# The recurrence's state products on the full array with zero blocks, and new places for buffers in SBUF

## The chip, the cores and the metric

One core of one Trainium2 chip runs the whole program. The time is the device time in microseconds, as the median of three runs. One execution more was taken with the hardware profiler, and the rows below come from it.

## The reference

Two blocks of a language model, in float32, over 256 tokens of width 2048. What matters here is the first block's recurrence (16 heads of 64, run as 8 pairs) and the large weight matrices around it.

```python
h = rms_norm(x, g_mix); proj = h @ w_in            # first projection, 60 units of 128 columns
y_dsa = dsa_mixer(q, k, v, q_idx, k_idx, w_idx)    # attention over selected keys
# recurrence, per head, over tokens t (state is 64 x 64)
def step(state, inp):
    sa = einsum('bhvk,bhk->bhv', state, -kk_t)
    state = state * w_t + sa[..., None] * b_t + v_t[..., None] * k_t
    return state, einsum('bhvk,bhk->bhv', state, r_t)
x = x + concat([y_dsa, y_rwkv]) @ w_out
x = x + hier_moe(rms_norm(x, g_ffn), ...)          # 16 experts, 2 of a group per token
# second block: projection, gates, three mixers, three branches, MLP with 4 * 2048 hidden
```

## The kernel before, in words

**Weights.** They come in units of 128 x 2048 floats through four ring slots (and, in the experts, two more). Each unit is split in two parts of fewer bits: ScalarE rounds it to a high part (`half_high`, L653, and `split_high`, L692), VectorE subtracts for the low part, in place (`half_low`, L658, and `split_low`, L699). The features are split likewise. A product of weights and features is three matmuls: high x high, high x low, low x high, 48 for a unit of 16 k-steps. Where the weights are loaded into the array and 256 columns of features stream, this is `split_unit` (L797, L799, L800) or, in the first projection, `product` (L855, L856, L857). Where the features are loaded and 512 columns of weights stream, it is `tokens_unit` (L823 to L825) and the expert products.

**Places.** All of this lies in one piece of SBUF that is taken by order: `ring`, `HT`, `YT`, `XT`, `C`, `SQ`, `work`. High parts of weights lie in `work`, `C`, `SQ` or `YT`, low parts in their slot. Features lie in `HT`, `YT`, `XT` or `work`. `H2_HI` and `H2_LO`, the MLP's input, lie in `work`.

**The recurrence.** It is done in chunks of 64 tokens, four for each of 8 pairs of heads. `pair(p)` on TensorE first makes scores, then inverts a triangular matrix by blocks (`sq2` to `inv64`), and then walks over the chunks c: `W` (state and keys), `U` (the inverse times W), `Z` (the change of the state), and the outputs of the chunk. Each is a product per head of 64 x 64, so two per pair, on the upper and the lower half of the array. W and U are copied by ScalarE (L1651, L1653) before the next product reads them. Z is taken by VectorE (L2236, L2238). `low_rank` makes the next pair's decays and gate (L896 to L899).

**The order.** It is written out by hand: `PE_RW`, `ACT_RW` and `DVE_RW` list the steps; each engine's queue follows them, and one semaphore per engine counts them. After each step TensorE runs a share of the first projection (`fill`), so that the wait for ScalarE or VectorE is covered. The shares are in `FILL`, 2 where none is given, and a cumulative sum turns them into whole k-steps, 96 for a pair (288 matmuls). When such a fill ends a half unit, ScalarE and VectorE have to round the next one, in their queues' order (`round_ahead`, `follow`). GpSimd does nothing until the first projection's later units are taken, then rotary products and, in the second block, tables.

Of the kernel before, what the change touches and what calls it, by code (L numbers as in the profile page):

```python
# [7 lines left out]
F32R = mybir.dt.float32r  # L8
# [291 lines left out]
FILL.update({f"{s}{c}": 1 for s in "WU" for c in range(NCH)})  # L300
FILL_FIRST = {"lora": 5, "kks": 14}
# [18 lines left out]
def build(nc, A, out):  # L320
    ctx = ExitStack()
    with ctx:
# [14 lines left out]
        ONEKA = sb("ONEKA", [P, 8])  # L337

        def split_memory(kind, suffix, pieces):
# [4 lines left out]
            shapes += [(f"work{i}", [P, n]) for i, n in enumerate(pieces)]  # L344
            with ExitStack() as c:
                return [c.enter_context(nc.sbuf_tensor(n + suffix, shape, kind)) for n, shape in shapes]
# [3 lines left out]
        def split_places(kind, suffix, pieces):  # L350

            shapes = [("ring", [P, RING, UNIT]), ("HT", [P, KT, T]), ("YT", [P, KT, T]), ("XT", [P, KT, T]),
                      ("C", [P, NC]), ("SQ", [P, 4, T])]
            shapes += [(f"work{i}", [P, n]) for i, n in enumerate(pieces)]
            with ExitStack() as c:
                return [c.enter_context(nc.sbuf_tensor(n + suffix, shape, kind)) for n, shape in shapes][6:]
# [3 lines left out]
        _, XG = split_places(F32R, "_tokens", [2 * PIECE, TILES * PIECE])  # L360
        PG = ctx.enter_context(nc.psum_tensor("PG", [P, BANKS, 512], F32))
# [78 lines left out]
        pool_chain = sem("pool_chain")  # L440
        g_in, g_sq, g_sum, g_ms, g_rt, g_vn, g_t, g_tt, g_mix, g_y = (sem("gmlp_" + n) for n in (
# [23 lines left out]
        ZB = cube(area(2 * CH), 2)  # L465
        ZP, W_, U_ = (area(CH) for _ in range(3))
        Y_, YC = area(T), area(T)
        ENDS = area(NCH)
        YSQ, G_IN = KK2, DA.rearrange("p n a -> p (n a)")
# [74 lines left out]
        GT = cube(area(3 * KT * T), 3 * KT)  # L544
        W_HI2_AT = taken[0]
# [3 lines left out]
        PW = [area(S5_TILES) for _ in range(5)]  # L549
        NEGM = area(P)  # L550
# [27 lines left out]
        H2_HI, H2_LO = rounded(gates_at + 2 * KT * T, KT), rounded(gates_at + KT * T, KT)  # L578
# [193 lines left out]
        def _(pe):  # L772
# [130 lines left out]
            def pair(p):  # L903
# [68 lines left out]
                for c in range(NCH):  # L972
# [35 lines left out]
                    if c + 1 == NCH:  # L1008
                        done(mm, p, f"Z{c}")
# [2005 lines left out]
```

## Time and profile before

| | us |
|---|---|
| median of three runs (lowest to highest) | 3074.66 (3071.51 to 3075.66) |
| profiled execution, its own time | 3069.26 |
| its span, first to last instruction | 3067.5 |
| TensorE, VectorE, ScalarE, GpSimd busy | 2964.6, 1918.2, 1532.9, 161.9 |

PE is TensorE's matmuls, PEld its weight loads, which overlap them; DVE is VectorE, ACT ScalarE and POOL GpSimd. A float32 product is recorded as two matmuls. Matmul durations overlap, so the start of the next one is what shows a product's price.

### The profile page before, as it was taken

Reading aid. Unit: us, or ns where it says so; the run is one execution under the profiler, and the core shown is the slowest. Engines: PE = TensorE matmul, PEld = TensorE weight load, DVE = VectorE, ACT = ScalarE, POOL = GpSimd, SP = SyncE. Lnnn points to the kernel's source line nnn. Section 1 sums busy time; section 2 is a strip of 40 time slices with the busy share of each in tenths; the row PEclk is TensorE's granted clock in tenths of the full one; section 3 lists DMA queues with packets and bytes.
Section 4 is the critical chain, followed back from the end, with each engine's and each line's share of the span. In section 5 each row is a group of like instructions: output and inputs, shape, how many; then the busy total and the mean of one; then the engine's idle time right before and its main releaser. Section 6 shows DMA issues by size and latency. Waiting matters only on the chain.

```text
span 3067.5 us, 52890 instructions
## 1 busy us (share of the span) xinstructions
PE 2964.6 (97%) x22088; PEld 2643.6 (86%) x22088; DVE 1918.2 (63%) x2591; ACT 1532.9 (50%) x2132; POOL 161.9 (5%) x248
## 2 busy tenths in 40 slices
PE   8999999879899999999899999999999999999998
PEld 7888888767688887777899999999989989898996
DVE  6555555874777877877759954445665545555454
ACT  5445444454566666665543347654344434344443
POOL 0000000200000000000075500000000000000000
PEclk9999999989899999999999999999999999999999
DMA  6223233223688888877444444445545555555554
GB/s 235 88 107 111 98 111 111 75 107 110 234 318 315 324 319 303 325 297 266 152 165 166 152 160 171 165 174 211 192 181 201 188 187 191 188 184 191 189 183 150
DMA packets 81955, 582.46 MB, mean 190 GB/s; under 512 B 9024, under 2 KB 9280, under 8 KB 12480
## 3 DMA queue, kind: packets, MB, share of 16 engines
q1 hardware_dynamic: 79056, 566.45, 50.0%
q10 hardware_dynamic: 2672, 12.71, 1.1%
q8 instruction: 175, 2.87, 0.4%
q14 instruction: 52, 0.43, 0.1%
HBM read 574.93 MB, written 4.19 MB: 189 GB/s over the span
## 4 chain that ended last, share of the span: by engine, by line
PE 86%; DVE 9%; ACT 2%; issue 1%; DMA 0%; ACTq 0%; SPq 0%; DVEq 0%
PE PG L799 10%; PE PG L797 10%; PE PG L800 10%; PE PG L824 6%; PE PG L825 6%; PE PG L823 6%; PE PG L855 4%; PE PG L1242 4%; PE PG L1243 4%; PE PG L1244 4%; PE PG L856 3%; PE PG L857 3%; DVE ring_r L699 3%; PE PX L942 2%; PE PX L1294 1%
## 5 line engine op out<-in xcount | busy, mean ns | idle before, releaser
L699 DVE TENSOR_TENSOR ring_r<-ring,work_r 128x1024 fp32r<-128x1024 f32 x492 | 584.0, 1230 | 313.8 <-ACT work_r L692 312.6
L692 ACT ACTIVATE work_r<-ring 128x1024 fp32r<-128x1024 f32 x492 | 493.0, 1051 | 537.8 <-PE PG L800 290.6
L692 ACT ACTIVATE C_r<-ring 128x1024 fp32r<-128x1024 f32 x268 | 269.1, 1052 | 419.1 <-PE PG L800 295.5
L800 PE MATMUL PG<-YT_r,ring_r 128*128 128x256 f32 x1664 | 469.1, 282 | 0.0
L699 DVE TENSOR_TENSOR ring_r<-ring,C_r 128x1024 fp32r<-128x1024 f32 x268 | 319.6, 1234 | 214.4 <-ACT C_r L692 213.2
L800 PE MATMUL PG<-work_r,ring_r 128*128 128x256 f32 x1344 | 374.8, 279 | 0.0
L800 PEld LDWEIGHTS PG<-YT_r,ring_r 128*128 128x128 f32 x1664 | 315.7, 190 | 0.0
L857 PE MATMUL PG<-HT_r,ring_r 128*128 128x256 f32 x960 | 271.1, 282 | 0.0
L800 PEld LDWEIGHTS PG<-work_r,ring_r 128*128 128x128 f32 x1344 | 253.3, 189 | 0.0
L824 PE MATMUL PG<-ring_r,HT_r 128*128 128x512 f32 x624 | 246.9, 396 | 0.0
L797 PE MATMUL PG<-YT_r,C_r 128*128 128x256 f32 x832 | 237.6, 286 | 6.4 <-DVE ring_r L699 6.4
L797 PE MATMUL PG<-YT_r,work_r 128*128 128x256 f32 x832 | 235.7, 283 | 5.9 <-DVE ring_r L699 5.9
L799 PE MATMUL PG<-HT_r,C_r 128*128 128x256 f32 x768 | 217.2, 283 | 0.0
L799 PE MATMUL PG<-HT_r,work_r 128*128 128x256 f32 x768 | 216.1, 281 | 0.0
L797 PE MATMUL PG<-work_r 128*128 128x256 f32 x672 | 188.8, 281 | 0.0
L797 PE MATMUL PG<-work_r,C_r 128*128 128x256 f32 x672 | 187.0, 278 | 0.0
L857 PEld LDWEIGHTS PG<-HT_r,ring_r 128*128 128x128 f32 x960 | 182.6, 190 | 0.0
L799 PE MATMUL PG<-work_r 128*128 128x256 f32 x640 | 179.8, 281 | 0.0
L799 PE MATMUL PG<-work_r,C_r 128*128 128x256 f32 x640 | 178.1, 278 | 0.0
L797 PEld LDWEIGHTS PG<-YT_r,C_r 128*128 128x128 f32 x832 | 159.5, 192 | 8.1 <-issue 7.6
L797 PEld LDWEIGHTS PG<-YT_r,work_r 128*128 128x128 f32 x832 | 158.9, 191 | 7.5 <-issue 7.0
L855 PE MATMUL PG<-HT_r,YT_r 128*128 128x256 f32 x480 | 153.7, 320 | 11.7 <-DVE XT_r L2040 11.7
(649 smaller groups left out, 7138.3 us busy)
## 6 DMA issues: line engine op xcount, KB each, us to landing
ring<-weights SPq DMA_DIRECT2D x472, 1024.0 KB, 4.8
C<-weights SPq DMA_DIRECT2D x32, 1024.0 KB, 4.8
work<-weights SPq DMA_DIRECT2D x32, 1024.0 KB, 5.1
work<-xT SPq DMA_DIRECT2D x4, 512.0 KB, 7.1
XT<-x ACTq DMA_DIRECT2D x1, 2048.0 KB, 10.0
residual<-XT ACTq DMA_DIRECT2D x4, 512.0 KB, 3.0
XT<-residual ACTq DMA_DIRECT2D x1, 2048.0 KB, 11.9
result<-YT SPq DMA_DIRECT2D x8, 256.0 KB, 2.9
```

The costliest lines, as they stand in the source:

```text
L692: act.activation(w_high(u)[:, c], weights(u)[:, c], ACT.Copy).then_inc(w_hi, 1)
L699: dve.tensor_tensor(w_low(u)[:, c], weights(u)[:, c], w_high(u)[:, c].bitcast(F32), ALU.subtract).then_inc(w_lo, 1)
L797: pe.matmul(o, wh, high[:, k, :], start=(n == 0 and not (down and t_ % 2)), stop=False, skip_group_check=True)
L799: pe.matmul(o, wh, low[:, k, :], start=False, stop=False, skip_group_check=True)
L800: last = pe.matmul(o, wl, high[:, k, :], start=False, stop=(n == kts - 1), skip_group_check=True)
L823: pe.matmul(o, xh, wh, start=(first and kk == 0), stop=False, skip_group_check=True)
L824: pe.matmul(o, xh, wl, start=False, stop=False, skip_group_check=True)
L825: mm = pe.matmul(o, xl, wh, start=False, stop=(last and kk == 3), skip_group_check=True)
L855: pe.matmul(o, wh, HT_r[:, k, :], start=(k == 0), stop=False, skip_group_check=True)
L857: mm = pe.matmul(o, wl, HT_r[:, k, :], start=False, stop=(k == KT - 1), skip_group_check=True)
L1242: pe.matmul(o, xh, wh, start=(k == 0), stop=False, skip_group_check=True)
L1243: pe.matmul(o, xh, wl, start=False, stop=False, skip_group_check=True)
```

## The change

1. W, U and Z of a chunk are each one product on 128 rows for both heads. The loaded operand is 128 x 128 with the two heads' 64 x 64 blocks on the diagonal and zeros elsewhere: `ARD`, `BTOKD`, `KTOKD`, `MKD`, `QD`. GpSimd clears these once at the start and copies the blocks for each pair; `QD` is written by VectorE, in two instructions for the last step of the inverse. TensorE waits for the copies before `W0`.
2. The outputs stay on 64 x 64 parts. Those of chunks 0, 1 and 2 are made after `W3`, those of chunk 3 as the last step. States `ZB` and `U_` are kept for all chunks. `FILL["W3"]` is 0.
3. The second product of the gate (`GUP`) loads all 128 rows in place of 32; the rows added are zero.
4. Gaps between buffers, and places of its own for the MLP's input; `PW` and `NEGM` move.

```diff
+FILL["W3"] = 0
+        sb("gap", [P, 8])
+        GAPS = (208, 0, 0, 48, 0, 176)      # floats before HT, YT, XT, C, SQ, work
+        H2_REST = 208
+        _, H2_LO_, H2_HI_ = split_places(F32R, "_hidden", [4 * PIECE + H2_REST, PIECE, PIECE])
-        H2_HI, H2_LO = rounded(gates_at + 2 * KT * T, KT), rounded(gates_at + KT * T, KT)
+        H2_LO, H2_HI = (cube(a, KT) for a in (H2_LO_, H2_HI_))
...
-                done(pe.matmul(PX[:, 2, T:2 * T], GUP[0:32, 1, cols], LO[0:32, 2, :], ...), p, "lora")
+                done(pe.matmul(PX[:, 2, T:2 * T], GUP[:, 1, cols], LO[:, 2, :], ...), p, "lora")
...
                 for c in range(NCH):
                     if c == 0:
                         dve(p, "q64")
+                        pe.wait_ge(s_blocks, 3 * p + 3)
                     else:
                         dve(p, f"z{c - 1}")
-                        for hs in HEADS:
-                            pe.matmul(PX[hs, 0, 0:CH], AR[hs, tt, 0, cs], z[hs, :], start=True, stop=False)
-                    for hs in HEADS:
-                        mm = pe.matmul(PX[hs, 0, 0:CH], MKK[hs, c, 0, :], VTOK_[hs, c, :], ...)
-                    done(mm, p, f"W{c}")
+                        pe.matmul(PX[:, 0, 0:CH], ARD[:, c - 1, :], ZB[:, c - 1, :], start=True, stop=False)
+                    done(pe.matmul(PX[:, 0, 0:CH], MKD[:, c, :], VTOK_[:, c, :], ...), p, f"W{c}")
+                    if c + 1 == NCH:
+                        for before in range(c):
+                            outputs(before)
                     act(p, f"W{c}")
-                    for hs in HEADS:
-                        mm = pe.matmul(PX[hs, 1, 0:CH], Q_[hs, c, :], W_[hs, :], start=True, stop=True)
+                    done(pe.matmul(PX[:, 1, 0:CH], QD[:, c, :], W_, start=True, stop=True), p, f"U{c}")
                     act(p, f"U{c}")
                     if c + 1 < NCH:
+                        pe.matmul(PX[:, 2, 0:CH], BTOKD[:, c, :], U_[:, c, :], start=True, stop=False)
+                        done(pe.matmul(PX[:, 2, 0:CH], KTOKD[:, c, :], VTOK_[:, c, :], ...), p, f"Z{c}")
+                    else:
+                        done(outputs(c), p, f"Z{c}")
...
+                    for h, hs in enumerate(HEADS):
+                        ins = dve.tensor_tensor(QD[hs, :, h * CH:h * CH + CH], Q_[hs], bank(b)[hs], ALU.add)
+                    done(ins, p, "q64")
...
         def _(pool):
+            for n, blocks in enumerate((ARD, BTOKD, KTOKD, MKD, QD)):
+                pool.memset(blocks, 0.0).then_inc(s_empty, 1)
+            pool.wait_ge(s_empty, 5)
+            for p in range(MT):
+                pool.wait_ge(DR.sem, DR.at(p, "ar"))       # then 4 copies into ARD
+                pool.wait_ge(AR_.sem, AR_.at(p, "tok"))    # then 4 copies into BTOKD, KTOKD
+                pool.wait_ge(DR.sem, DR.at(p, "mk"))       # then 2 copies into MKD
```

## Rows read from the trace of the kernel before

**Rows 1.** The page, part 1: busy us, share of the span, instructions.

```profile
PE 2964.6 (97%) x22088; PEld 2643.6 (86%) x22088; DVE 1918.2 (63%) x2591; ACT 1532.9 (50%) x2132; POOL 161.9 (5%) x248
```

**Rows 2.** TensorE in time in the fourth pair: start us, us, line, out<-in; W0, U0, Z1.

```profile
270.88 0.33 PE L984 MATMUL PX<-work 64*64 64x64 f32 x4
271.14 0.39 PE L855 MATMUL PG<-HT_r,YT_r 128*128 128x256 f32 x1
271.36 0.28 PE L856 MATMUL PG<-XT_r,YT_r 128*128 128x256 f32 x1
...
271.84 0.28 PE L857 MATMUL PG<-HT_r,ring_r 128*128 128x256 f32 x1
272.05 0.33 PE L988 MATMUL PX<-work 64*64 64x64 f32 x4
...
273.44 0.33 PE L993 MATMUL PX<-work 64*64 64x64 f32 x4 [0.51 <-ACT work L1653]
...
273.82 0.39 PE L855 MATMUL PG<-HT_r,work_r 128*128 128x256 f32 x1
```

**Rows 3.** ScalarE in time beside it: copy of W, rounding of a half unit.

```profile
271.26 0.23 ACT L1651 ACTIVATE work<-PX 128x64 f32<-128x64 f32 x1 [2.04 <-PE PX L984]
272.22 1.06 ACT L653 ACTIVATE YT_r<-ring 128x1024 fp32r<-128x1024 f32 x1 [0.73 <-PE PG L857]
```

**Rows 4.** TensorE in time: the gate's two products, and a product alone in the fill.

```profile
276.45 0.70 PE L898 MATMUL PX<-work 128*128 128x256 f32 x2
...
277.71 0.39 PE L855 MATMUL PG<-HT_r,work_r 128*128 128x256 f32 x1
...
278.88 0.60 PE L901 MATMUL PX<-work,C 128*128 128x256 f32 x2
...
279.44 0.28 PE L856 MATMUL PG<-XT_r,SQ_r 128*128 128x256 f32 x1
```

**Rows 5.** TensorE in time, experts: float32 records on the full array with few columns.

```profile
812.51 1.50 PE L1213 MATMUL PX<-work,work_r 128*128 128x5 f32 x12
813.87 0.48 PE L1242 MATMUL PG<-HT_r,work_tokens 128*128 128x512 f32 x1
```

**Rows 6.** VectorE in time, fourth pair: step "mk", and the inverse's last sum.

```profile
249.40 0.76 DVE L2203 TENSOR_TENSOR work<-PX,C 128x256 f32<-128x256 f32 x2 [0.99 <-PE PX L924]
...
269.37 0.42 DVE L2225 TENSOR_TENSOR work<-work,PX 128x256 f32<-128x256 f32 x1 [1.46 <-PE PX L942]
```

**Rows 7.** Groups of GpSimd: count, busy us, mean ns, idle before; its copies.

```profile
L2877 POOL COPY work<-work 128x32 f32<-128x32 f32 x1 | 1.2, 1183 | 943.5 <-DVE work L2635 943.5
...
L2884 POOL COPY XT<-work 128x32 f32<-128x32 f32 x2 | 0.5, 240 | 0.1
```

**Rows 8.** TensorE in time: starts of units of 48 products, gates and MLP.

```profile
2049.73 0.28 PE L797 MATMUL PG<-YT_r,work_r 128*128 128x256 f32 x1
...
2055.38 0.28 PE L797 MATMUL PG<-YT_r,C_r 128*128 128x256 f32 x1
...
2061.14 0.28 PE L797 MATMUL PG<-YT_r,work_r 128*128 128x256 f32 x1
...
2351.15 0.28 PE L797 MATMUL PG<-work_r,C_r 128*128 128x256 f32 x1
...
2356.59 0.28 PE L797 MATMUL PG<-work_r 128*128 128x256 f32 x1
...
2362.24 0.28 PE L797 MATMUL PG<-work_r,C_r 128*128 128x256 f32 x1
...
2529.02 0.28 PE L797 MATMUL PG<-work_r,C_r 128*128 128x256 f32 x1
...
2551.64 0.28 PE L797 MATMUL PG<-work_r,C_r 128*128 128x256 f32 x1
```

**Rows 9.** TensorE in time: end of a unit whose products stream 512 columns.

```profile
2338.84 0.40 PE L825 MATMUL PG<-work_r,HT_r 128*128 128x512 f32 x1
2339.07 0.28 PE L797 MATMUL PG<-work_r,C_r 128*128 128x256 f32 x1
```

More of the change, by code:

```diff
@@ L344, in split_memory @@
             shapes += [(f"work{i}", [P, n]) for i, n in enumerate(pieces)]
+            spaced = []
+            for i, shape in enumerate(shapes):
+                spaced += [(f"gap{i}", [P, GAPS[i - 1]])] if 1 <= i <= len(GAPS) and GAPS[i - 1] else []
+                spaced.append(shape)
+            return spaced
+        def split_memory(kind, suffix, pieces):
             with ExitStack() as c:
-                return [c.enter_context(nc.sbuf_tensor(n + suffix, shape, kind)) for n, shape in shapes]
+                all_of_them = [(n, c.enter_context(nc.sbuf_tensor(n + suffix, shape, kind))) for n, shape in places(pieces)]
+                return [tensor for n, tensor in all_of_them if not n.startswith("gap")]
         def split_places(kind, suffix, pieces):
-            shapes = [("ring", [P, RING, UNIT]), ("HT", [P, KT, T]), ("YT", [P, KT, T]), ("XT", [P, KT, T]),
-                      ("C", [P, NC]), ("SQ", [P, 4, T])]
-            shapes += [(f"work{i}", [P, n]) for i, n in enumerate(pieces)]
             with ExitStack() as c:
-                return [c.enter_context(nc.sbuf_tensor(n + suffix, shape, kind)) for n, shape in shapes][6:]
+                all_of_them = [(n, c.enter_context(nc.sbuf_tensor(n + suffix, shape, kind))) for n, shape in places(pieces)]
+                return [tensor for n, tensor in all_of_them if not n.startswith("gap")][6:]
         ring, HT, YT, XT, C, SQ, work = split_memory(F32, "", [WORK])
@@ L464, in build @@
         TM, GM = D2T, DT
-        ZB = cube(area(2 * CH), 2)
-        ZP, W_, U_ = (area(CH) for _ in range(3))
+        ZB = cube(area((NCH - 1) * CH), NCH - 1)
+        ZP, W_ = area(CH), area(CH)
+        U_ = cube(area(NCH * CH), NCH)
         Y_, YC = area(T), area(T)
         ENDS = area(NCH)
+        ARD, BTOKD, KTOKD = (cube(area((NCH - 1) * P), NCH - 1) for _ in range(3))
+        MKD, QD = (cube(area(NCH * P), NCH) for _ in range(2))
         YSQ, G_IN = KK2, DA.rearrange("p n a -> p (n a)")
@@ L544, in build @@
         GT = cube(area(3 * KT * T), 3 * KT)
+        NEGM = area(P)
+        PW = [area(S5_TILES) for _ in range(4)]
         W_HI2_AT = taken[0]
@@ L548, in build @@
          S_LAR, S_MAG2, S_KR2, S_KI2) = (area(S5_TILES) for _ in range(19))
-        PW = [area(S5_TILES) for _ in range(5)]
-        NEGM = area(P)
+        PW.append(area(S5_TILES))
         area(0, gates_at)
@@ L898, in low_rank @@
                 pe.matmul(PX[:, 2, T:2 * T], GUP[:, 0, cols], LO[:, 1, :], start=True, stop=False)
-                done(pe.matmul(PX[:, 2, T:2 * T], GUP[0:32, 1, cols], LO[0:32, 2, :], start=False, stop=True), p, "lora")
+                done(pe.matmul(PX[:, 2, T:2 * T], GUP[:, 1, cols], LO[:, 2, :], start=False, stop=True), p, "lora")
                 act(p, "kk2")
@@ L1652, in pair @@
                     pe(p, f"U{c}")
[L1653 removed]
+                    done(act.activation(U_[:, c, :], PX[:, 1, 0:CH], ACT.Copy), p, f"U{c}")
                     if c == 0 and ahead:
```

62 lines of the change are left out of this document (37 added, 25 removed).

## The prediction

> **What bounds the kernel now.** I read the page's busy shares first, then the order of time of TensorE, ScalarE and VectorE inside one pair of heads of the recurrence (the fourth of eight, whose neighbours repeat it), then the starts of the large products in the later stages. TensorE is busy 97% of the span [rows 1]; no other engine is above 63%. So what TensorE issues, and how far apart its products start, is the time. A matmul's recorded duration (279 to 286 ns for 256 columns) is no price, because matmuls overlap; the price is the distance from one start to the next.
>
> In a pair, 96 steps of the projection's fill (three products of 256 columns each) are dealt out between the small products of the recurrence. Each small product is two matmul records for each head on a 64x64 part of the array. A visit from the fill to one such product (W0) takes 0.26 us (270.88 to 271.14); the first fill product after it takes 0.22 (271.14 to 271.36) where the ones inside the fill take 0.12, and the last one before the next visit 0.21 (271.84 to 272.05) [rows 2]. So one visit of four records costs 0.26 + 0.10 + 0.09 = 0.45 us. A visit of eight records (Z1) has 0.38 us from start to start of the next fill, 0.57 with its edges; four records more cost 0.12. So of 0.45 us only 0.12 are products and 0.33 are for coming and going between 128x128 and 64x64 work.
>
> PE also waits twice in a pair, behind U1 and behind U3: 0.51 us before Z1, released by ScalarE's copy of U [rows 2]. ScalarE was not short of time: its rounding of a half unit (1.06 us) stands ahead of that copy in its queue [rows 3].
>
> **The recurrence.** Products of W, U and Z now have 128 rows and columns, one product for both heads, two records. No row of before has exactly this shape in this place. Nearest: twelve records on 128x128 with five columns, 812.51 to 813.87, so 113 ns a record [rows 5]; the weights' load sets that, not the columns. From below, a record cannot be less than the 64x64 ones, 30 ns; from above, four times 64 columns of work at the price of 256 columns (0.44 us for two records, see lora) would be 0.22 a record. I take 113, the nearest in shape, so 0.226 for a product, without edges, because the mode does not change.
> - W0 and U0 to U3: 5 visits from 0.45 to 0.226: 1.12 us.
> - W1, Z0, Z1, Z2: 4 visits of eight records, 0.57 to 0.45 (two products): 0.48 us.
> - W2 and W3 stood in one visit with the outputs of the chunk before. Outputs 0 to 2 are now one 64x64 visit between W3 and U3: 32 records at 30 ns = 0.95, and 0.33 of coming and going; with W2 and W3 at 0.45 each that is 2.18. Before, the same was 20 records twice (0.59 + 0.33 each) and outputs 0 ahead of the lora (0.24): 2.08. Loss: 0.10.
>
> Sum 1.5 us a pair, 12 us for eight. The 17 products have 34 records: at 30 ns each that is 34 x 83 = 2.8 us more gain a pair, at 220 ns 3.6 less, so a loss of 2.1.
>
> GUP's second product gets 128 rows in place of 32. The gate's two products take 1.26 us from 276.45 to 277.71, 1.36 with the edge. A 256-column product with 128 rows, alone in the fill, has 0.56 from its start to the second fill product (278.88 to 279.44), less 0.12: 0.44 [rows 4]. Two make 0.88: 0.48 saved, in 7 pairs: 3 us (between 0, if the edge before them stays, and 3.4).
>
> **The share of the fill.** W3 gets none, so the cumulative sum moves by a step here and there. Worked out from the code for pairs 1 to 6: W3 2 to 0, W0 2 to 1, U0 1 to 2, U3 1 to 2, sq4 5 to 6 and so on; still 96. The ends of half units leave W3 and now fall into the fill behind W0, U1, U2 and U3. The wait before Z3 should go (two steps, 0.71 us, cover a copy like W's, which begins 0.38 us after its product's start and takes 0.23 [rows 2, 3]); the one near Z0 stays, about 0.45, plus 0.1 where one step covers W's copy. Each is at most 0.51 to 0.58 us a pair: I take 3 us in all, from 0 to 8. After W3 the outputs themselves (1.3 us) cover W's copy. Late next is nothing: inv64's sum now is two VectorE instructions; the one of before runs at 269.37 for 0.42 and W0 starts at 270.88 [rows 2, 6], so 1.1 us of slack for 0.42 more. If that cover were gone it would cost 0.4 a pair.
>
> **GpSimd.** Ten copies a pair, and W0 waits for the last. The last depends on "mk", done by 250.16, 20.7 us ahead of W0 [rows 2, 6]. A copy of 128x32 took 240 ns at one place and 1183 at another [rows 7]. Ten at 1183 are 12 us, and wider ones (up to 256 columns) perhaps twice that for the worst; at 240 to 800 they are 3 to 6 us. Nothing else is queued on GpSimd then, and in program order its rotary products come after pair 7. I take zero; bounds 0 and 5 us. The five clearings run at the start, long before QD is wanted.
>
> So the recurrence part is 12 + 3 + 3 = 18 us.
>
> **The places in memory.** The gaps move starts within 1 KB. From the shapes: before, ring, HT, YT, XT and C start at one remainder of 1024 bytes and the work area 320 bytes past it. After, ring, C and work are at 0, HT, YT, XT and the two H2 halves at 832. Weights step 512 bytes from k to k, features 1024, so a distance d is read as d and d + 512 in turn. What rows show for 48 products of 256 columns [rows 8]:
> - features and both weights' parts at one remainder (distance 0; gates, weights in C): 2055.38 to 2061.14, 120.0 ns a product;
> - high part 704 away, low part 0 (gates, weights in work): 2049.73 to 2055.38, 117.7;
> - 320 away in all (MLP, weights in C): 2351.15 to 2356.59, 113.3;
> - high part at 0, low at 320 (MLP, weights in work): 117.7 (2356.59 to 2362.24);
> - the same two kinds in the second MLP block: 192 products from 2529.02 to 2551.64, 117.8.
>
> So the start-to-start distance depends on where things lie, and the same places gave 113.3 once and 117.8 another time. The new distance is 832, and 832 with its alternate (832 + 512 = 320 mod 1024) is the pair 320 and 832: what "320 in all" already reads, in the other order. I therefore expect no third speed but one of these two, 113.3 or 117.8. I take 116.5, between, nearer the second, since I found three MLP blocks of four there and show one. The 96 units of the second projection and the 8 of the second branch are 104 x 48 = 4992 products, now at 118.9 (the mean of 120.0 and 117.7): -2.4 ns, -12 us. The MLP's first halves are 64 x 48 = 3072 at 117.2 (115.5 in one block, 117.8 in three): -2 us. The first projection's 60 units, 2880 products at 0.12 [rows 2], keep distance 0 for the high parts in YT and get 832 for the low ones: -2 us. The first and third branches, whose features stay in the work area, come to distance 0: 768 products, +2.5 us. Products of 512 columns start 0.23 us apart (2338.84 to 2339.07 [rows 9]); there the weights stream and the features load, and the trace's resolution in these rows is 10 ns. I take zero, with 5 us either way for some 5200 of them (1 ns each). Together -14. Ends: all at 113.3: -28 -12 -6 +2 = -44; all at 117.8: -5.5 +2 -3 +1 = -5.5; all at 120: +17.
>
> The Trainium skill says the opposite of all this: TensorE: Matmul & The Clock Gate (Part 2) gives TensorE two independent SBUF read ports, so that loading the next weights takes nothing from the running matmul, and SBUF — State Buffer (Who interferes with whom) has TensorE never waiting on anyone. By that, places would change nothing and the time would be 3074.7 - 18 = 3057. The rows above disagree: 113.3 against 120.0 ns for one shape [rows 8]. It is within rival 1 all the same.
>
> For the visits, TensorEngine Tiling (Array Packing), Key Properties, says that a change of tiling mode drains the engine, and its section on when to tile recommends 64x64 tiles for contractions of up to 64. By the second alone (products only, 0.12 against 0.226 us) the change would lose 17 x 0.107 = 1.8 us a pair; by the first it wins the 1.5 above, and the trace agrees with the first: 0.33 us a visit beside 0.12 of products [rows 2].
>
> **Sum.** The profiled execution took 3069.3 us (span 3067.5 and 1.8 around it). 3069.3 - 18 - 14 = 3037. The median of the three timed runs, 3074.7, lies 5.4 above it, so the forecast for the time is 3074.7 - 32 = 3042.
>
> **Rivals.**
> 1. The placement gives nothing (products settle at 117.8, or nothing in the streams depends on it): 3074.7 - 18 and 0 to 5 more, 3055. For: three blocks of four at 117.8. Against: the gates with weights in C, at 120.0, have most to gain.
> 2. The placement finds 113.3 nearly everywhere: 3074.7 - 18 - 44 = 3013. For: 113.3 was reached with these distances in rows 8. Against: the second block shows them at 117.8.
> 3. The new distance is worse than any seen: the 256-column streams go to 120 (+17 us) and the 512-column ones get slower by the same 2%, 4.6 ns x 5200 = +24, so 3074.7 - 18 + 41 = 3098, slower. It decides against the change once the streams lose 18 us, 1.1 ns on each of some 16000 products. For: 832 was not run. Against: the equality with 320 above.
> 4. The zero blocks save nothing: a record costs 0.22 rather than 0.113 us, or GpSimd's copies hold VectorE. With 0.22 the recurrence loses 2.1 us a pair in place of winning 1.5, 29 us in all: 3042 + 29 = 3071. If VectorE's chain were held by copies, 3 us a pair would give 3042 + 24 = 3066; the copy of 1183 against 240 ns [rows 7] is the only sign. The Trainium skill (SBUF — State Buffer, Who interferes with whom) says that a VectorE instruction with two SBUF inputs and a GpSimd one that reads SBUF exclude each other; no row of before shows the two side by side in a pair.
>
> **Chances.** Forecast 0.56, rival 1 0.20, rival 2 0.12, rival 3 0.05, rival 4 0.07. Within 0.2% is within 6 us, about what a measurement can tell. Faster: forecast, 1 and 2 all but a little, and half of 4: 0.88; same 0.05; slower 0.07. The range takes in rivals 1 and 2 nearly, from 3010 to 3064; the forecast's own range is 3028 to 3054.
>
> **What would show it.** In a pair, W0 and U0 each with two records of 128x128 about 113 ns apart, and 0.12 us for the first fill product after them; the wait before Z3 gone; each pair shorter by 2 to 2.5 us. GpSimd done with "mk" copies 10 us or more ahead of W0. In the gates, 48 products in 5.44 or 5.65 us in place of 5.76. Wrong would be: the first fill product after W0 at 0.22, records 0.2 apart, PE waiting before W0 for GpSimd, or gates at 120 and more.

## The result, and the profile after

| us | before | changed |
|---|---|---|
| median (lowest to highest, runs) | 3073.09 (3071.25 to 3075.66, 4) | 3051.77 (3050.28 to 3052.53, 4) |
| profiled execution's span | 3067.5 | 3049.4 |

The ratio is 0.9932, 95% interval 0.992 to 0.9945: faster by 21 us. The forecast was 3042, 32 us faster; the measured time lies in its range, and 3 us below rival 1 (the placement gives nothing, 3055). A time alone cannot tell the two apart. So I read the trace stage by stage before believing either.

The page's first part after the change, which answers to [rows 1]: TensorE has 272 records fewer and is still busy 97% of the span; GpSimd has 55 us more.

```profile
PE 2949.3 (97%) x21816; PEld 2645.3 (87%) x21816; DVE 1922.2 (63%) x2599; ACT 1532.5 (50%) x2132; POOL 216.5 (7%) x333
```

Busy time of each stretch, before: the pairs of the recurrence, the last part of attention (its first part, between the two, lasts 56.7 us in both kernels), the rest of the first block (output projection, router and experts, called "the experts" from here on), the second projection with gates and branches, the MLP. Columns: window, its length, busy us and instructions of PE, PEld, DVE, ACT, POOL, granted clock of TensorE as a share of 2.4 GHz, DMA share, GB/s.

```profile
62.30:543.20 480.90, 468.75 (x5806) 416.91 (x5807) 259.53 (x497) 222.02 (x410) 0.00 (x0) 0.99 0.29 104
599.90:672.20 72.30, 54.72 (x305) 41.66 (x304) 55.62 (x191) 36.23 (x97) 0.00 (x0) 0.87 0.25 91
672.20:1471.40 799.20, 769.87 (x3395) 615.91 (x3395) 586.94 (x659) 482.23 (x571) 0.00 (x0) 0.98 0.72 274
1471.40:2342.56 871.16, 858.58 (x7323) 831.84 (x7322) 550.83 (x651) 424.08 (x549) 141.02 (x219) 1.00 0.48 174
2342.56:3067.50 724.94, 713.45 (x4587) 645.88 (x4585) 376.56 (x435) 301.07 (x408) 0.00 (x0) 0.99 0.51 185
```

The same stretches after:

```profile
61.90:520.70 458.80, 450.73 (x5531) 418.69 (x5532) 264.21 (x505) 221.31 (x410) 52.14 (x80) 1.00 0.31 109
577.35:652.30 74.95, 57.27 (x305) 43.12 (x304) 55.61 (x191) 36.11 (x97) 0.00 (x0) 0.85 0.24 88
652.30:1450.50 798.20, 768.94 (x3393) 615.72 (x3394) 586.70 (x659) 481.90 (x571) 0.00 (x0) 0.98 0.72 274
1450.50:2320.30 869.80, 855.76 (x7323) 829.26 (x7322) 550.21 (x652) 424.53 (x550) 141.31 (x219) 1.00 0.49 174
2320.30:3049.40 729.10, 717.65 (x4587) 646.84 (x4585) 376.49 (x435) 301.18 (x407) 0.00 (x0) 0.99 0.52 184
```

Attention begins 22.5 us earlier. After that the start of each later stage tells what was added or given back: +2.6 in the last part of attention (no instruction differs there; in the stretch of 72.30 and 74.95 us the granted clock is 0.87 and 0.85, so more of it ran at 1.2 GHz; among the kernels further down, too, this stretch is 2.3 us longer in some, whatever their places), -1.0 in the experts, -1.4 in the second projection, **+4.2 in the MLP**. The recurrence gave more than the 18 us predicted, and the placement, priced at -14, gave nothing in sum; the run with the placement alone shows that.

**Inside a pair.** The fourth pair, from one pair's start to the next: 60.60 us before with 1.02 in which PE did nothing, and 57.65 with 0.21. First row before, second after.

```profile
240.00:300.60 60.60, 59.58 (x738) 53.03 (x737) 33.28 (x64) 28.73 (x54) 0.00 (x0) 1.00 0.29 106
```

```profile
231.25:288.90 57.65, 57.44 (x704) 53.44 (x703) 33.86 (x65) 28.60 (x54) 6.84 (x10) 1.00 0.32 111
```

TensorE in time around W0, U0 and Z0 of that pair, after (answers to [rows 2]): start, duration, line, out<-in, and idle before.

```profile
262.10 0.29 PE L875 MATMUL PG<-HT_r,ring_r 128*128 128x256 f32 x1
262.22 0.33 PE L1014 MATMUL PX<-work 128*128 128x64 f32 x2
262.36 0.36 PE L873 MATMUL PG<-HT_r,YT_r 128*128 128x256 f32 x1
262.56 0.28 PE L874 MATMUL PG<-XT_r,YT_r 128*128 128x256 f32 x1
...
262.87 0.43 PE L1019 MATMUL PX<-work 128*128 128x64 f32 x2
263.11 0.37 PE L873 MATMUL PG<-HT_r,work_r 128*128 128x256 f32 x1
...
263.79 0.28 PE L875 MATMUL PG<-HT_r,ring_r 128*128 128x256 f32 x1
264.27 0.43 PE L1022 MATMUL PX<-work 128*128 128x64 f32 x2 [0.21 <-ACT work L1671]
```

The entry from the fill costs nothing now: 262.10 to 262.22, where it was 0.21. W0's two records take 0.14, and the first fill product after them 0.20 where 0.12 is normal. So the product is 0.14 + 0.08 = 0.22 us, for a predicted 0.226; before, it was 0.45. U1 and U2 cost the same 0.22, and the visits with two products (W1, W2, Z1, Z2) 0.44.

The sum came, but not as it had been split. The fill product behind W0 was to take 0.12, and the prediction had named 0.22 there a sign of being wrong: it takes 0.20. So 0.08 us of the 0.33 "for coming and going" stays although the mode no longer changes, and W0's two records reach the next start in 0.14 where 0.226 had been expected. In a visit with two products the two records more do cost what was said: 0.44 less 0.22 is 0.22, 0.11 each.

The wait near Z0 is still there, in two parts. Before Z0: 0.48 from the last fill product to Z0, less 0.12, and Z0's visit itself is 0.11 longer than Z1's (0.47 for 0.36), so 0.48 in all. Before U0: 0.19 into it where 0.12 is normal, and 0.24 to the next fill product where U1 takes 0.14, so 0.17; the profile shows no idle time there, since a matmul before it is still recorded as running. Together the waits cost 0.65 us in this pair. Before the change they cost 0.58 at Z0 and 0.58 at the outputs of chunk 3, 1.17 in all, priced in the same way.

The outputs of chunks 0 to 2 in one visit between W3 and U3, after:

```profile
279.94 0.33 PE L999 MATMUL PX<-work 64*64 64x64 f32 x4
...
281.02 0.43 PE L1019 MATMUL PX<-work 128*128 128x64 f32 x2
281.26 0.36 PE L873 MATMUL PG<-HT_r,YT_r 128*128 128x256 f32 x1
```

From 279.94 to 281.02 is 1.08 us, and U3 follows without a wait. GpSimd's copies of the same pair are these (first rows and last; the ten take 6.84 us):

```profile
225.99 0.23 POOL L2880 COPY work<-work 64x64 f32<-64x64 f32 x1 [40.47 <-DVE work L2200]
226.17 1.38 POOL L2881 COPY work<-work 64x128 f32<-64x128 f32 x1
...
241.41 1.77 POOL L2891 COPY work<-work 64x256 f32<-64x256 f32 x2 [3.83 <-DVE work L2221]
```

They end at 243.18, 19 us ahead of W0 at 262.22. A copy of one shape takes 0.30 us or 1.38 here. VectorE in the same stretch shows what is beside the long one, the subtraction that makes a half unit's low part, with both inputs in SBUF:

```profile
226.18 1.22 DVE L676 TENSOR_TENSOR ring_r<-ring,YT_r 128x1024 fp32r<-128x1024 f32 x1
```

All 30 copies that take 0.8 us or more in the eight pairs overlap such a subtraction; copies of the same shapes away from one take 0.30 to 0.40. It is mostly GpSimd that is held: VectorE's subtraction keeps its 1.22 us, but for one in most pairs (235.98) that takes 1.38. TensorE's waits in the pair are for ScalarE, so nothing of this reaches it.

**The streams.** Starts of units of 48 products of 256 columns in the gates, then in the MLP, then of 24 products of 512 columns in the MLP, after:

```profile
2031.00 0.28 PE L815 MATMUL PG<-YT_r,C_r 128*128 128x256 f32 x1
2036.65 0.28 PE L815 MATMUL PG<-YT_r,work_r 128*128 128x256 f32 x1
...
2328.88 0.28 PE L815 MATMUL PG<-work_hidden,C_r 128*128 128x256 f32 x1
2334.53 0.28 PE L815 MATMUL PG<-work_hidden,work_r 128*128 128x256 f32 x1
...
2464.03 0.39 PE L841 MATMUL PG<-C_r,HT_r 128*128 128x512 f32 x1
2469.63 0.39 PE L841 MATMUL PG<-work_r,HT_r 128*128 128x512 f32 x1
```

Gates: 5.65 us for the unit with weights in C, 117.7 ns a product, and as much for the one in work behind it (to 2042.30); in [rows 8] they were 120.0 and 117.7. MLP: 5.65, where its first block had 5.44 in [rows 8]. Products of 512 columns: 5.60 for 24, 233.3 ns. Before, 48 of them took 11.11 us, 231.5 ns:

```profile
2473.26 0.40 PE L823 MATMUL PG<-C_r,HT_r 128*128 128x512 f32 x1
...
2484.37 0.40 PE L823 MATMUL PG<-C_r,HT_r 128*128 128x512 f32 x1
```

The prediction had set these products at zero change. Their three kinds do not lie at one distance in either kernel: before, one kind of three is at 320 and two at 0; after, the two that load `HT` are at 832, and the one that loads the features' low part, in `work`, is at 0.

### The profile page after: what moved, and what is told of

Read it like the earlier page. It is cut to its first block, busy times and chain, and to the rows that moved or that the text cites. A ratio compares the mean times of both kernels' runs of the same rounds, so it can differ in the third digit from the quotient of the medians.

```text
span 3049.4 us, 52456 instructions
## 1 busy us (share of the span) xinstructions
PE 2949.3 (97%) x21816; PEld 2645.3 (87%) x21816; DVE 1922.2 (63%) x2599; ACT 1532.5 (50%) x2132; POOL 216.5 (7%) x333
## 4 chain that ended last, share of the span: by engine, by line
PE 86%; DVE 10%; ACT 2%; issue 1%; DMA 0%; ACTq 0%; SPq 0%; DVEq 0%
PE PG L815 10%; PE PG L817 10%; PE PG L818 10%; PE PG L843 6%; PE PG L841 6%; PE PG L842 6%; PE PG L873 4%; PE PG L1260 4%; PE PG L1262 4%; PE PG L1261 4%; PE PG L874 3%; PE PG L875 3%; DVE ring_r L717 3%; PE PX L960 2%; PE PX L1313 1%
## 5 line engine op out<-in xcount | busy, mean ns | idle before, releaser
L818 PE MATMUL PG<-work_hidden,ring_r 128*128 128x256 f32 x1024 | 285.7, 279 | 0.0
L818 PEld LDWEIGHTS PG<-work_hidden,ring_r 128*128 128x128 f32 x1024 | 192.3, 188 | 0.0
L841 PE MATMUL PG<-work_r,HT_r 128*128 128x512 f32 x368 | 146.7, 399 | 3.9 <-DVE ring_r L717 3.9
L817 PEld LDWEIGHTS PG<-HT_r,C_r 128*128 128x128 f32 x768 | 144.7, 188 | 0.0
L817 PEld LDWEIGHTS PG<-HT_r,work_r 128*128 128x128 f32 x768 | 144.0, 188 | 0.0
L815 PE MATMUL PG<-work_hidden,C_r 128*128 128x256 f32 x512 | 143.3, 280 | 0.0
```

The costliest lines, as they stand in the source:

```text
L815: pe.matmul(o, wh, high[:, k, :], start=(n == 0 and not (down and t_ % 2)), stop=False, skip_group_check=True)
L817: pe.matmul(o, wh, low[:, k, :], start=False, stop=False, skip_group_check=True)
L818: last = pe.matmul(o, wl, high[:, k, :], start=False, stop=(n == kts - 1), skip_group_check=True)
L841: pe.matmul(o, xh, wh, start=(first and kk == 0), stop=False, skip_group_check=True)
```

## The experiments

The theory: the recurrence's products carry the whole gain, and the places help some streams and hurt others. The rival: the placement works as predicted, and something in the changed recurrence gives it back. Each time is a median with its lowest and highest, and each ratio is to the kernel before, measured beside it (the median of that kernel moved between 3071.1 and 3073.8, so times of different experiments are compared by the ratios where 2 us matter).

**The recurrence alone** (all gaps zero, the MLP's input where it was):

```diff
-        GAPS = (208, 0, 0, 48, 0, 176)
+        GAPS = (0, 0, 0, 0, 0, 0)
```

> The whole change but without the gaps and the new places of the MLP's input: every buffer at its old remainder. Theory A (the recurrence is the whole gain, its eight pairs are 22.5 us shorter, and the new places cost 0 to 4 us, mostly in the MLP): 3046 to 3051 us, 0 to 5 us below the changed kernel's 3051.8, MLP stage 725 us long as in the kernel before. Theory B (the places earn part of the 21 us): slower than the changed kernel, 3056 or more. Both: a pair's period 57.6 to 57.8 us.

3054.06 (3048.86 to 3055.08), ratio 0.9941 (0.9927 to 0.9955). The pair's period is 57.89 us, 2.72 less than before's 60.61. The time lies between the two theories, 3 us above A's range and 2 below B's, and the period is 0.1 over the range of both. Eight pairs give 21.8 us, but the span of the profiled execution fell by 14.6 only, though no instruction behind the recurrence differs from before. Some 3.5 us of the rest are in the first 40 us of the second projection, where the granted clock is 0.91 (1.00 before), and 1.5 are in the first block of the MLP. There the units with weights in C, at 5.44 us in [rows 8], take 5.66 with the same places:

```profile
2335.03 0.28 PE L812 MATMUL PG<-work_r,C_r 128*128 128x256 f32 x1
...
2340.69 0.28 PE L812 MATMUL PG<-work_r 128*128 128x256 f32 x1
```

So it is not the places that decide between 113.3 and 117.8 ns.

**The placement alone** (the kernel before, and of the change only this, with the move of `PW` and `NEGM`):

```diff
+        GAPS = (208, 0, 0, 48, 0, 176)
+        H2_REST = 208
-        H2_HI, H2_LO = rounded(gates_at + 2 * KT * T, KT), rounded(gates_at + KT * T, KT)
+        H2_LO, H2_HI = (cube(a, KT) for a in (H2_LO_, H2_HI_))
```

> The kernel before with the gaps and the new places of the MLP's input alone; the recurrence as it was. Theory A: 0 to 4 us slower than the kernel before, 3073 to 3077; gates at 117.8 ns a product in place of 120.0 and 117.7, MLP at 117.8 in all four blocks, its 512-column products near 233.3 ns in place of 231.5, first and third branch at 120.0. Theory B: 3 us or more faster than before, 3070 or less.

3070.85 (3067.70 to 3076.24), ratio 1.0000 (0.9991 to 1.0009). The prices of the streams came as theory A said, but the time did not get longer; it lies between A's range and B's. So the places are worth nothing, within 3 us, and the recurrence alone makes the changed kernel's time but for 2 to 3 us (0.9941 beside 0.9932, whose intervals overlap). By stage, the placement alone gave -2.7 us up to attention (pair period 60.33) and +4.3 in the MLP. Of that, 1.5 us came with the recurrence alone as well (the first block's 5.65), so 2.8 are the placement's. The rival falls: the placement has nothing to give back.

**Outputs in each chunk again, with the share of before** (zero blocks and places kept):

```diff
-FILL["W3"] = 0
+FILL["W3"] = 1
-                    if c + 1 == NCH:
-                        for before in range(c):
-                            outputs(before)
                     act(p, f"W{c}")
...
+                    if c + 1 < NCH:
+                        outputs(c)
                     if c == 0 and p + 1 < MT:
```

> The changed kernel with each chunk's outputs again after its Z, and W3's share of the fill back to 1; products on 128 rows and places as changed. Theory A (coming and going between 64x64 and 128x128 work is the price, about 0.33 us): two visits to the 64x64 part more per pair, and outputs 0 joins the gate's visit: 0.3 to 0.7 us a pair slower, so 3054 to 3058. Rival (order does not matter, only the number of small products): the same 3051.8 within 1.5 us.

3064.33 (3062.81 to 3066.02), ratio 0.9978 (0.9968 to 0.9987): 12.6 us above the changed kernel. Its pair lasts 59.37 us, 1.72 more, where theory A had 0.3 to 0.7. Two long waits are back in each pair, before Z0 and before the outputs of chunk 3. TensorE in this kernel:

```profile
266.68 0.28 PE L875 MATMUL PG<-HT_r,ring_r 128*128 128x256 f32 x1
267.70 0.43 PE L1019 MATMUL PX<-work 128*128 128x64 f32 x2 [0.75 <-ACT work L1670]
...
286.25 0.28 PE L875 MATMUL PG<-HT_r,ring_r 128*128 128x256 f32 x1
287.27 0.33 PE L996 MATMUL PX<-work 64*64 64x64 f32 x4 [0.75 <-ACT work L1670]
```

ScalarE in the same stretch: the copy of W, the rounding of a half unit (1.06 us), and behind it the copy for which PE waits.

```profile
265.65 0.22 ACT L1668 ACTIVATE work<-PX 128x64 f32<-128x64 f32 x1 [1.91 <-PE PX L1014]
266.48 1.06 ACT L671 ACTIVATE YT_r<-ring 128x1024 fp32r<-128x1024 f32 x1 [0.60 <-PE PG L875]
267.44 0.21 ACT L1670 ACTIVATE work<-PX 128x64 f32<-128x64 f32 x1
```

From 266.68 to 267.70 is 1.02 us for a product of 0.12, and Z0's visit is 0.11 longer than Z1's: a wait of 1.0. The one at 287.27 costs 0.8 (1.02 for the usual 0.21 at such an entry). Together 1.8 us, where the changed kernel has 0.65: that is 1.2 us of the 1.72. The other 0.5 are the visits that theory A had counted; the waits were what it left out.

**The share alone back** (only the first two lines of that diff).

> The changed kernel with W3's share of the fill back to 1 (outputs of chunks 0 to 2 still between W3 and U3). The ends of half units fall behind W0 and W3 again. Theory (shorter visits uncover ScalarE's rounding; the wait behind U0 is 0.65 us as changed, about 1.0 with one step behind U0; behind W3 the outputs cover it): 0.3 to 0.6 us a pair slower, pairs of 57.9 to 58.3 us, time 3053 to 3057. Rival (the order of the outputs alone made the 12.5 us of the run with outputs per chunk, the share nothing): 3051.8 within 1.5.

3053.37 (3052.93 to 3054.17), ratio 0.9941 (0.9926 to 0.9956); pair 58.06 us, so 0.41 of the 1.72 is the share and 1.31 the order of the outputs. Pair and time are in the theory's ranges. The wait near Z0 costs 1.0 us again (263.01 to 264.04, with 0.75 idle for ScalarE's copy, L1671), 0.36 more than the changed kernel's 0.65. The wait behind U3 is not back: it makes 0.8 of the 1.31 of the order, and the visits make 0.5.

**The last wait covered** by a second step behind U0, taken from the one behind "tok":

```diff
 FILL["W3"] = 0
+FILL["U0"] = 2
+FILL["tok"] = 3
```

> The changed kernel with two shares of the fill behind U0 and three in place of four behind the turned tokens, so that no half unit ends behind a W and W0, U0 cover two and three steps. Theory: the last wait of a pair, 0.17 + 0.48 us before U0 and Z0, goes: pairs of 57.0 to 57.2 us in place of 57.65, 4 to 5 us in all: 3047. Rival (another wait takes its place, in the scores behind the shorter tokens' fill): 3051.8 within 1.5 us.

3051.49 (3050.38 to 3055.73), ratio 0.9933 (0.9919 to 0.9947): no change, as the rival had it; pair 57.59, 0.06 less. The waits before U0 and Z0, 0.65 us, are gone, and one before the scores has come, behind the step that was made shorter, for VectorE (235.52 to 236.33, 0.60 over the usual 0.21):

```profile
235.52 0.28 PE L877 MATMUL PG<-HT_r,ring_r 128*128 128x256 f32 x1
236.33 0.47 PE L950 MATMUL PX<-work 64*64 64x64 f32 x9 [0.53 <-DVE work L2207]
```

**GpSimd's copies made twice** (each group of copies is run, waited for and run again, before its semaphore is raised).

```diff
+                    for again in range(2):
                         for h, hs in enumerate(HEADS):
...
+                        else:
+                            ins.then_inc(once, 1)
+                            pool.wait_ge(once, 3 * p + g + 1)
```

> The changed kernel with GpSimd making each of a pair's copies twice, one set after the other (about 14 us of GpSimd per pair in place of 7). Theory (copies are hidden, some 20 us ahead of W0, and hold VectorE by too little to reach TensorE): pairs of 57.65 us, 3051.8 within 1.5 us. Rival (they take turns with VectorE's two-input instructions in the inverse's chain and cost some us now): 2 us or more slower, by as much as they cost once.

3051.84 (3050.20 to 3055.38), ratio 0.9939 (0.9924 to 0.9954), pair 57.65 as in the changed kernel: the copies are hidden even twice. What the run does not double is their meeting with VectorE: there are 30 long copies in it, as in the changed kernel, and the fourth pair has 10.3 us of GpSimd for 6.8. That this meeting costs nothing rests on the changed kernel's trace, where VectorE loses 0.16 us in a pair and TensorE does not wait for VectorE.

**Features at 512 bytes in place of 832**, the MLP's input too. All operands of a product then start at one remainder of 512 bytes:

```diff
-        GAPS = (208, 0, 0, 48, 0, 176)
+        GAPS = (128, 0, 0, 128, 0, 176)
-        H2_REST = 208
+        H2_REST = 128
```

> The changed kernel with the features 512 bytes past the weights (mod 1024) in place of 832: gaps of 128 and 128 floats for 208 and 48, MLP's input likewise. Theory (what counts is the distance mod 512 in the streams where k moves the weights by 512 bytes, so 512 is the same as 0): gates, second branch and the MLP's first halves at 120.0 ns a product in place of 117.8, 8064 products, 15 to 19 us slower in the second block and 3 us in the pairs: 3068 to 3073. Rival (512 is a distance of its own, or the trace's spacing does not follow places): 117.8 or 113.3, 3052 or less.

3043.72 (3042.85 to 3045.74), ratio 0.991 (0.9895 to 0.9925): 8 us **faster** than the changed kernel. My expectation was wrong in its sign, and this run shows what the term that the prediction had put at zero, the 512-column products, is worth. Starts in this kernel:

```profile
2027.13 0.28 PE L815 MATMUL PG<-YT_r,C_r 128*128 128x256 f32 x1
...
2032.89 0.28 PE L815 MATMUL PG<-YT_r,work_r 128*128 128x256 f32 x1
...
2471.07 0.39 PE L841 MATMUL PG<-C_r,HT_r 128*128 128x512 f32 x1
...
2476.51 0.39 PE L841 MATMUL PG<-work_r,HT_r 128*128 128x512 f32 x1
```

A unit of 256-column products takes 5.76 us (120.0 ns each) as I had said. 24 products of 512 columns take 5.44 in place of 5.60: 226.7 ns in place of 233.3. The experts' stage, which is mostly made of them, falls by 13.7 us (652.30 to 1450.50 was 798.20):

```profile
653.10:1437.60 784.50, 755.27 (x3394) 613.45 (x3395) 586.64 (x659) 481.67 (x571) 0.00 (x0) 0.98 0.74 279
1437.60:2316.40 878.80, 867.76 (x7323) 842.98 (x7322) 551.62 (x651) 424.29 (x550) 140.02 (x219) 1.00 0.49 173
2316.40:3041.80 725.40, 714.25 (x4587) 653.94 (x4585) 376.24 (x435) 300.99 (x407) 0.00 (x0) 0.99 0.52 185
```

The second projection loses 9.0 us, the MLP gains 3.7 (its 1536 products of 512 columns gain 6.6 ns each, 10, and its 3072 of 256 lose 2.2, 7). So the 256-column streams are slower here and the 512-column ones faster. That these are slower at 64 bytes as such is not shown: in this kernel all three kinds of a unit lie at 0 or 512, while in the changed one two are at 832 and one at 0, and no kernel here has all three at 832. It may be the mixture that costs.

**Each stream at its own place:** gap of 512 bytes as above, the MLP's input at 832.

```diff
-        GAPS = (208, 0, 0, 48, 0, 176)
+        GAPS = (128, 0, 0, 128, 0, 176)
```

> The buffers at rest 0 and 512 bytes (the gap of 128 floats), but the MLP's input at 832 bytes, as in the changed kernel. Theory (256-column streams take 120.0 ns where rest modulo 512 is 0 and 117.8 where it is 320; 512-column streams take 226.7 ns where it is 0, 231 or more where it is not; each depends on its own pair of places only): against the run with 512 bytes everywhere (span 3041.8 us) only the MLP's first halves change, 64 units x 48 x 2.2 ns = -6.8 us, so a span of about 3035 us and a time of 3037. Rival (the 512-column streams of the MLP were fast because its input lay at 512 too, or the fast state belongs to the whole layout): MLP's 512-column products return to 233 ns, +4 us, and the time is 3041 to 3044.

3038.49 (3037.20 to 3041.09), ratio 0.9888 (0.9872 to 0.9905), span 3035.4, as the theory had it to 0.4 us. The MLP's first halves are at 5.66 a unit again, its second halves stay at 5.44, the stage takes 718.7:

```profile
2330.93 0.28 PE L815 MATMUL PG<-work_hidden,work_r 128*128 128x256 f32 x1
...
2336.59 0.28 PE L815 MATMUL PG<-work_hidden,C_r 128*128 128x256 f32 x1
...
2469.74 0.39 PE L841 MATMUL PG<-C_r,HT_r 128*128 128x512 f32 x1
...
2475.18 0.39 PE L841 MATMUL PG<-work_r,HT_r 128*128 128x512 f32 x1
```

By the ratios it beats the changed kernel by 13 us and the one before by 34.

**Other distances.** Gaps of 512 and the MLP's input at 256; then all features at 256; then gaps of 512 and the MLP's input at 128.

```diff
+        GAPS = (128, 0, 0, 128, 0, 176)     # first
+        H2_REST = 64
...
+        GAPS = (64, 0, 0, 192, 0, 176)      # second
+        H2_REST = 64
...
+        GAPS = (128, 0, 0, 128, 0, 176)     # third
+        H2_REST = 32
```

> As the kernel with the gap of 512 bytes, but the MLP's input at rest 256 bytes. A scan of one more distance for 256-column streams. Theory (some multiple of 64 bytes modulo 512 decides, 320 gives 117.8 or 113.3): no rule for 256; if what counts is an offset of half the period it is the farthest from 0 and gives 113.3 ns (MLP's first halves 5.44 us a unit, 20 us less than at 120.0). Rival (only 0 is special): 117.8, like 320, time 3037.

3048.12 (3048.01 to 3048.22, 2 runs), ratio 0.9917 (0.9897 to 0.9937). Neither speed came: at 256 the MLP's first halves are at 120.0 ns, and the stage takes 725.4 as at 512: 256 is no better than 0.

> The gap is 256 bytes for the features' buffers and the MLP's input. Theory (512-column streams are fast only at rest modulo 512 = 0): experts and MLP second halves back at 231 ns or more, +14 and +4 us against the 512-byte kernel; 256-column streams at whatever the MLP's input at 256 shows, 117.8 or 113.3. So at 117.8 a time like the changed kernel's, 3050; at 113.3 3020 to 3030. Rival (512-column streams are fast at multiples of 256): 226.7 ns and a time of 3028 to 3035 with 256-column streams at 117.8.

3044.06 (3043.79 to 3044.33, 2 runs), ratio 0.9904 (0.9884 to 0.9924). Every stage is as long as with 512, experts 784.5, MLP 725.4: for both kinds of stream 256 counts as 512 does. The theory fell, and the rival was right on the 512-column streams.

> As the kernel with rest 0 and 512 and the MLP's input apart, but that input at rest 128 in place of 832. A scan of the last distance modulo 256 that was not seen: 0 and 256 gave 120.0 ns, 832 (64 modulo 256) 117.8. Theory (half the period of 256 bytes is the farthest from 0): 113.3 ns in the MLP's first halves, 64 x 48 x 4.5 = -14 us against the kernel at 832, span 3021. Rival (whatever is not 0 modulo 256 gives 117.8): span 3035, as at 832. Second rival (128 is itself a period): 120.0 and a span of 3042.

3045.04 (3042.71 to 3047.37, 2 runs), ratio 0.9915 (0.9895 to 0.9935). At 128 the MLP's first halves are at 118.7 ns in the first block and at 119.9 to 120.0 in the three others; half a period is not best. The second rival (128 is itself a period) nearly came: its span was 3042, and 3 us of the 3045.3 are the experts, which took 787.5, not 784.5, in this kernel and in the one at 256 in the MLP alone, with the same places there. The clock fits that: from 1150 to 1170 us the granted clock is 0.91 in these two and 1.00 in the kernel with the MLP's input at 832, and from 780 to 800 us 0.77 and 0.78 for 0.88.

**YT and XT at 832, HT at 512:**

```diff
-        GAPS = (208, 0, 0, 48, 0, 176)
+        GAPS = (128, 80, 0, 48, 0, 176)
```

> As the last kernel (buffers at rest 0 and 512, the MLP's input at 832), but YT and XT at 832 in place of 512; HT stays at 512. Features of the gates: the high part (two products of three) lies in YT, the low part in HT. Theory (what counts is the distance of a product's own two operands modulo 256 bytes, 0 or 64): the gates' 104 units go from 120.0 to 117.8 in two products of three at least, 3328 x 2.2 ns = -7 us (all three, -11); experts whose operands lie partly in YT, some 500 products of 512 columns, lose up to 5 ns each, +2.5. Span about 3030 to 3032, against 3035.4; time 3034. Rival (a unit is fast only if all three kinds lie at one distance): gates stay at 120.0 and the experts lose, time 3040 to 3042.

3038.28 (3034.06 to 3038.82), ratio 0.9894 (0.9877 to 0.991): no different from the kernel it was made from (3038.49); the forecast was 3034. The gates did get faster, in part. TensorE in time:

```profile
2031.02 0.28 PE L815 MATMUL PG<-YT_r,work_r 128*128 128x256 f32 x1
...
2036.72 0.28 PE L815 MATMUL PG<-YT_r,C_r 128*128 128x256 f32 x1
```

5.70 us for 48 is 118.8 ns. Taken over a unit by line, the two products with YT are 117.3 from start to start and the one with HT, which stayed at 512, 122.1 and not 120.0. So a product's price is not set by its own distance alone: in a mixture, the one at distance 0 costs more than in a stream that is all at 0, and that takes some 40% of the gain back. The stage gained 4.3 us, where 7 to 11 had been expected, and the experts, whose operands partly lie in YT, lost 5.0, twice the forecast.

## Why the prediction was right or wrong

**The visits: right.** 1.6 us a pair was predicted for the zero blocks before the outputs' 0.10 of loss. Priced by starts in the fourth pair, W0 and the four U give 1.19 (1.12 predicted; U0 without its wait), W1 and the three Z 0.52 (0.48). W0 has 0.22 for 0.226, the entry is free as said, and the visits with two products take four records in 0.36 and 0.08 after, 0.44. The split was wrong: the way back costs 0.08 still, and the first two records cost less than 113 ns each. The choice between 30 and 220 ns a record, from the nearest shape [rows 5], held. The Trainium skill (TensorEngine Tiling (Array Packing), Key Properties) has the drain at a change of tiling mode. The trace agrees here too: 0.22 us without a change of mode against 0.45 with one, for the same two 64 x 64 products, though the number of records is halved as well. What the prediction took from the page's section on when to tile was too wide: there the Trainium skill (TensorEngine Tiling (Array Packing), When to Use Tiling) has row tiling for a contraction of up to 64 and column tiling for a left operand of up to 64 columns, and only the two together make 64x64 tiles.

**The outputs: small, with the wrong sign.** From the end of the fill to its first product behind U3 plus the edge, W3, outputs and U3 take 1.89 us (279.46 to 281.26, 0.09 more); the prediction's terms make 0.45 + 0.95 + 0.33 + 0.23 = 1.96. Before, the outputs of chunk 0 ahead of the gate cost 0.38, not 0.24 (1.01 us to the gate's first product, 0.63 after). So W2, W3 and the three outputs take 2.11 us after and took 2.22 before: a gain of 0.1 in place of a loss of 0.10.

**The gate: 0.39 a pair** in place of 0.48 (its two products start at 266.96 and 267.50 and the second fill product behind them at 268.06).

**The fill shares and waits: right in size.** I gave 3 us in all, 0.4 a pair, for one wait that goes and one that stays. The wait before the outputs of chunk 3 went as said, and that near Z0 stayed, 0.65 us with U0's part where I had written 0.45 and perhaps 0.1 more. The waits fell from 1.17 to 0.65, by 0.5 us. (The profile's idle time fell by more, from 1.02 to 0.21, because it does not show U0's.) What I did not see is how much hangs on the order of the outputs. I booked it as a loss of 0.10 a pair; against outputs in each chunk on the same zero blocks, with the share of before, it is a gain of 1.31: 0.8 because the outputs cover ScalarE's rounding and copy of W3, so that the wait behind U3 goes, and 0.5 of visits. The share gives 0.41 more. The visits, the outputs, the gate and the waits come to 1.7 + 0.1 + 0.4 + 0.5 = 2.7 us, for a predicted 2.25; the recurrence alone showed 2.72 a pair and the kernel with places 2.96.

**GpSimd: right,** shown by the run with double copies. That copies and VectorE hold each other, the premise of rival 4, does occur: a copy of 64x128 takes 1.38 us beside VectorE's subtraction and 0.30 away from it. But it costs VectorE 0.16 us in a pair, off TensorE's path, and not the 3 us that the rival needed.

**The places: the step that failed.** It said -14 us, most of it in the second projection, and zero for 512 columns. Measured by the placement alone: none, within 3 us.
- That 832 reads as 320 (832 + 512 = 320 modulo 1024) held: one of the two known speeds came, 117.8. I took 116.5, between them. The 113.3 came in few places only, and the MLP's first block lost it. It lost it with the old places too (the recurrence alone), so rival 2, and the part of my 116.5 that leaned on it, rested on something that the places do not decide.
- Second projection: 5.5 us are due at 117.8 against 118.9, where I had 12, less 2 in the branches; the stage shows 1.4. Of the 2 us between, some 1.6 are the clock: in the first 40 us of the stage it is granted 0.96, and 1.00 before. The first projection's 2 us did come (0.28 a pair with the placement alone).
- 512 columns were not at zero: 231.5 to 233.3 ns in the MLP. With 1536 such products there, 1.8 ns are 2.8 of the 4.2 us by which that stage grew; the first block's first halves, 5.44 to 5.65, are the rest, and are not the placement's. And the 3 to 5 ns a product that all kinds at 0 or 512 would have won were not thought of. Inside my bounds of 5 us, but taken as nothing because these rows differ by 1 to 2 ns where their resolution is 10. A unit of 24 would have told.

So what rival 1 described is what happened, at 3 us less than its number, because the recurrence gave more. With the 18 us as forecast and nothing from the places, the time would have been 3056.7 (3074.7 - 18), outside the forecast's own range of 3028 to 3054. That it lies inside is luck: the recurrence gave 3.8 us more (8 times 2.72 is 21.8), and with a fourth run the median of the kernel before is 1.6 us lower (3073.1). Up to attention 18 us and 2 of the places were forecast, and 22.5 came. In the later stages -12 was forecast, and they took 4.4 more (2.6 of them in the last part of attention, by the clock). Together that is the 13.9 us by which the span's -18.1 misses -32. By the medians it is 10.7, since the profiled execution of before lay below its median and that of after did not. Rivals 2 and 3 fell: the streams are at 117.8, neither at 113.3 nor at 120 (of rival 3 only the slower 512-column products came, by 0.8% in the MLP). Rival 4 fell with the visits, the double copies and VectorE's 0.16 us.

The Trainium skill (TensorE: Matmul & The Clock Gate, Part 2) has the weights' load and the stream on two independent read ports. That places would then not matter is what the prediction drew from it, and this does not hold: the same 512-column products come at 226.7 and 233.3 ns, the same 256-column ones at 117.7 and 120.0, by places alone. Whether the ports are where it happens, no run here shows.

## What to carry to other kernels

Where TensorE goes back and forth between full-array work and 64x64 products, zero blocks on the diagonal can be cheaper than the change of mode: here 0.22 for 0.45 us. Work that waits for nothing (outputs of earlier chunks) belongs in front of the wait, since here what covered ScalarE's copy was worth more than it cost. Where a placement is tuned by the streams that one looks at, measure the others as well, over whole units. Here the places that helped the 256-column products slowed the 512-column ones; a layout chosen by both took off 13 us more than the change's own. And compare stages by their granted clock before a difference of 1 to 4 us is put down to code: several here went with the clock.

## What the runs showed of the hardware

The start-to-start distance of matmuls depends on how far the loaded and the streamed operand's starts are apart, by a period of 256 bytes or less. The weights alone or the features alone were moved, with the same effect on the gates (117.7 ns for 120.0); no stream has all its operands moved together, so the distance is the likely reading and not a proven one.

- 256 columns, all three kinds of a unit at 0, 256 or 512: 120.0 ns. All at 832: 117.8. With one or two kinds at 64 modulo 256: 117.7 to 118.8. At 128: 118.7 in one block of the MLP, 119.9 to 120.0 in three.
- 512 columns, all kinds at 0, 256 or 512: 226.7 ns. With one kind of three at 320, 231.5; with two at 832, 233.3. All three at 64 modulo 256, or at 128, was not run.
- 113.3 ns for 256 columns, all at 320, came in one block of the kernel before and, with the same places, not in the run with the recurrence alone (117.8). What decides it stays open, as does what in the chip makes places matter.

A GpSimd copy from SBUF to SBUF (0.30 to 0.40 us) takes 1.16 to 1.38 us beside a VectorE subtraction of 1.22 us with both inputs in SBUF. The subtraction takes 1.38 us where the copy was under way first.
